# Loading ten triples of experts per layer in two parts instead of whole

## The reference

```python
scores = sigmoid(einsum('td,de->te', xf, router_w))          # 256 tokens, 64 experts
_, idx = top_k(scores + router_b, 6)
wts = sel / sum(sel) * 2.5                                   # sel: the six chosen scores
hid = silu(xb @ w_gate[e]) * (xb @ w_up[e])                  # w_gate, w_up: 1024 x 256
ys  = (hid @ w_down[e]) * w                                  # w_down: 256 x 1024
out = sum over a token's six experts + the shared expert
```

## Time and profile before

| | |
|---|---|
| median of 3 runs | 1425.58 us (1424.98 to 1426.55) |
| the profiled execution, its own time | 1425.3 us |
| its span, first to last instruction | 1423.5 us |
| TensorE matmul busy | 1266.5 us (89%) |
| HBM read | 496.57 MB |
| first layer's experts, about | 300 to 760 us |
| second layer's experts, about | 960 to 1416 us |

### The profile page before, as it was taken

One profiled execution on the slowest core, in us unless ns is written; L12 is line 12 of the kernel. 1 busy time (PEld: TensorE's weight loads), 2 busy tenths in 40 slices (PEclk: granted clock), 3 DMA queues, 4 the chain that ended last, 5 costly groups with the idle time before them and its releaser, 6 DMA issues.

```text
span 1423.5 us, 23092 instructions
## 1 busy us (share of the span) xinstructions
PE 1266.5 (89%) x9704; PEld 723.7 (51%) x9704; DVE 608.7 (43%) x1131; ACT 273.6 (19%) x464; POOL 59.9 (4%) x112
## 2 busy tenths in 40 slices
PE   5999888999998879888798999999999788977887
PEld 1445335775554444434446766875555344443444
DVE  5998872254433221222324687763433212222222
ACT  3226341321111110111112113131111101111111
POOL 0010581000000000000000000000000000000000
PEclk9999999999999999999999999989999999999999
DMA  9674865969999999999999962678999999999996
GB/s 380 241 206 88 161 196 213 392 262 395 422 423 421 430 429 426 427 428 428 423 417 344 390 261 89 240 336 333 401 423 421 422 432 428 426 428 428 427 422 271
DMA packets 54763, 502.85 MB, mean 353 GB/s; under 512 B 9788, under 2 KB 16700, under 8 KB 22588
## 3 DMA queue, kind: packets, MB, share of 16 engines
q1 hardware_dynamic: 54108, 499.18, 87.3%
q10 hardware_dynamic: 544, 2.10, 0.4%
HBM read 496.57 MB, written 4.69 MB: 352 GB/s over the span
## 4 chain that ended last, share of the span: by engine, by line
PE 54%; DMA 36%; DVE 6%; SPq 1%; issue 1%; ACT 1%; DVEq 0%; ACTq 0%
PE ps L790 52%; DMA arena<-in_w_experts 29%; DMA arena<-in_ada_w 7%; PE ps L461 2%; SPq L508 1%; ACT arena L1455 1%; DVE arena L2267 1%; DVE arena L2175 0%; DVE arena L1908 0%; PE ps L843 0%; DMA arena<-in_mcst 0%; DVE arena L1921 0%; PE ps L1055 0%; DVE arena L2257 0%; DVE arena L2256 0%
## 5 line engine op out<-in xcount | busy, mean ns | idle before, releaser
L790 PE MATMUL ps<-arena 128*32 128x512 f32 (+10 forms) x9192 | 1209.9, 457 | 137.9 <-DMA arena<-in_w_experts 55.0
L790 PEld LDWEIGHTS ps<-arena 128*32 128x32 f32 (+6 forms) x9192 | 691.8, 139 | 644.4 <-issue 493.8
L1455 ACT ACTIVATE arena<-ps 128x512 f32<-128x512 f32 (+6 forms) x261 | 142.1, 545 | 928.2 <-PE ps L790 880.5
L2117 DVE SCALAR_TENSOR_TENSOR arena<-arena,ps 128x256 f32<-128x256 f32 x44 | 21.1, 481 | 272.9 <-ACT arena L1455 272.9
L1455 ACT ACTIVATE arena<-arena 128x256 f32<-128x256 f32 (+7 forms) x143 | 94.0, 682 | 153.8 <-DVE arena L2135 58.2
L2133 DVE CAST arena<-ps 128x512 bf16<-128x512 f32 x42 | 29.0, 691 | 164.0 <-PE ps L790 164.0
L2077 DVE COPY arena<-ps 128x512 f32<-128x512 f32 x44 | 30.4, 691 | 132.2 <-PE ps L790 132.2
L2105 DVE TENSOR_TENSOR arena<-arena 128x1024 bf16<-128x1024 f32 x42 | 51.5, 1225 | 37.3 <-ACT arena L1455 37.0
L2135 DVE TENSOR_TENSOR arena<-ps,arena 128x1024 f32<-128x1024 f32 x42 | 51.4, 1224 | 1.4
L780 POOL MEMSET arena<- 128x1 f32 x2 | 0.2, 100 | 1165.3 <-PE ps L790 1165.3
L461 PE MATMUL ps<-arena 128*24 128x512 f32 x256 | 33.3, 621 | 3.3 <-DMA arena<-in_ada_w 3.3
(11 more groups left out here) (233 smaller groups left out, 471.1 us busy)
## 6 DMA issues: line engine op xcount, KB each, us to landing
arena<-in_w_experts SPq DMA_DIRECT2D x70, 3072.0 KB, 22.0
arena<-in_w_experts SPq DMA_DIRECT2D x80, 1024.0 KB, 13.1
arena<-in_w_experts SPq DMA_DIRECT2D x38, 2048.0 KB, 21.5
arena<-in_ada_w SPq DMA_DIRECT2D x34, 1024.0 KB, 6.8
arena<-in_ada_w SPq DMA_DIRECT2D x7, 2048.0 KB, 19.0
arena<-in_hy_w_in SPq DMA_DIRECT2D x6, 2048.0 KB, 15.4
arena<-in_w_experts SPq DMA_DIRECT2D x6, 1536.0 KB, 20.7
arena<-in_w_experts SPq DMA_DIRECT2D x18, 512.0 KB, 22.8
```

The costliest lines, as they stand in the source:

```text
L790: return pe.matmul(out, lhsT, rhs, start=start, stop=stop, skip_group_check=skip)
L1455: return act.activation(out, in_, func, **kw)
L2117: stt(hh, sg, wtab[:, n:n + 1], ps[:, GU, FF:2 * FF], M, M).then_inc(sem("h_done"), 1)
```

## The change

`whole(t)` is false for every triple. SP therefore takes the path of `half_loads` for triples 8 to 17 too, in both layers: 60 transfers of 3 MB become 60 of 2 MB and 60 of 1 MB. Bytes, slots, matrix products and the work of VectorE and ScalarE stay the same.

```diff
         def whole(t):
 
-            return LATE <= t < TRIPLES - 2
+            return False
```

## The result

Five runs after the change have a median of 1432.19 us (1431.16 to 1433.88); five of the kernel before, 1426.55. The ratio is 1.0035 with a 95% interval of 1.002 to 1.005: 5.0 us, 2.9 to 7.1 (it is estimated from all ten runs; the two medians alone are 5.6 us apart). The forecast was 1431.5 us, slower, in a range of 1428 to 1435.

What follows compares the result with a forecast made beforehand. The prediction took the full transfer queue, for which TensorE waits, as the bound. 3.0 us per layer gave 1425.3 + 6.0 = 1431.3 us profiled, and 1431.5 us as the median, in a range of 1428.0 to 1435.0.

Steps and rivals of the forecast that it cites:

- The queue sets the pace: Triples 9 to 17: transfers, not TensorE, set the 22.16 us per triple, so added transfer time reaches the end.
- the sum: Whole kernel: 3.0 us more per layer, both on the path, 6.0 us in all.
- The price by rates, 5.2 us, and by landings, 7.2: 60 split expert loads: 0.087 us each by window rates, 0.12 us each by landing intervals; 6.0 us taken in all.
- SP's issues and the earlier release cost and gain nothing: SP's queue: sixty more issues of 0.52 us are not waited for; earlier issues only join a full queue.
- The new wait before down products: TensorE, within a triple: down parts land 7.6 us after gate and up parts, with 1.8 us to spare; no cost.
- The lead is given back: Triples 8 to 17 start first products some 7.6 us earlier against the queue; not kept at triples 18 and 19.
- The start of triple 19 is set by the queue in both kernels: Last triple of each layer: waits for its weights before and after the change, with the same work following.
- Triple 19 near 748 and 1406: Last triple's start: about 3 us later in the first layer (748), 6 us later in the second (1406).
- No change (1): Split loads of triples 8 to 17: the parts cost nothing, 1425.6 to 1426.6 us; chance 13%.
- Holes in the queue (2): Start of whole triples: late whole loads starve the queue, so earlier issues make it faster, 1399.8 us; chance 6%.
- The interval of 23.51 us (3): Triples in parts: one slow interval in the second layer is the rule, much slower, 1452.6 us; chance 7%.
- The lower clock (4): Last triple of each layer: TensorE starts at the lower clock, 1.7 us more per layer, 1434.9 us; chance 9%.

Runs made afterwards that it cites:

- the padded rows: Kernel before, experts stored with padding so that one transfer moves two 12 KB pieces per partition: 1431.5 us against 1428.8, ratio 1.0031.
- two transfers: Kernel before, each whole load of triples 8 to 17 sent as an even-partition and an odd-partition transfer: 1429.06 us against 1428.8, ratio 1.0003.

## Why the prediction was right, step by step

- *The queue sets the pace.* Right: DMA share 1.01 after, and 22.47 in place of 22.16 us per triple; over 20 triples 6.2 us, near the 6.0 of the sum. The timed interval, 2.9 to 7.1 us, holds both.
- *The price by rates, 5.2 us, and by landings, 7.2.* The windows after give 422 GB/s, 3.146 / 0.422 = 7.455 us per expert and 0.097 more than whole: 5.8 us, between the two. The landings agree: from the last part of triple 7 to the last of triple 17, 30 experts took 221.99 and 221.21 us in the two layers before and 225.05 and 224.09 after, 5.9 us more (6.0 with the padded rows, 1.3 with two transfers). The sum stands. What the prediction left open was what in the change the price is of; the two runs that separate them show that it is the pieces of a partition's row, not the transfers.
- *SP's issues and the earlier release cost and gain nothing.* Right, and shown: sixty more issues with whole rows change nothing that shows, and neither does holding the parts back.
- *The new wait before down products.* Right. TensorE's waits for weights from 512 to 710 and from 1156 to 1354 (us, times, longest):

```profile
PE ps L790 <- DMA arena<-in_w_experts: 13.9, 8, 2.8
...
PE ps L790 <- DMA arena<-in_w_experts: 8.3, 5, 2.7
```

  The timeline has each of them at the start of a triple's gate and up products (0.35 at triple 10 to 1.02 at triple 17), none before down products.

- *The lead is given back.* Right: 8.88 and 8.51 us at triple 18.
- *"The start of triple 19 is set by the queue in both kernels."* This step was too sure. Triple 19 came when forecast, 748 and 1406, but without a wait: after its long wait triple 18's stretch took 14.29 and 14.83 us where it took 12.96, at a granted clock of 0.75 and 0.67 of full speed at its start, so partly at the lower of the two levels, 1.2 and 2.4 GHz. A window of each layer after:

```profile
729.60:735.00 5.40, 5.40 (x40) 1.49 (x44) 0.00 (x0) 0.00 (x0) 0.00 (x0) 0.75 1.02 425
1387.30:1393.00 5.70, 5.70 (x36) 1.45 (x40) 0.00 (x0) 0.00 (x0) 0.00 (x0) 0.67 1.03 423
```

  The same place of the second layer before:

```profile
1381.00:1386.00 5.00, 5.00 (x48) 1.56 (x52) 2.46 (x3) 1.06 (x1) 0.00 (x0) 1.00 1.03 424
```

  That used up the slack of 1.13 and 1.61 us before triple 19. The last part that triple 19's first products need was issued at 715.32 and 1373.40 and took 32.9 and 32.5 us to land, at 748.2 and 1405.9. In the first layer TensorE comes just as it lands, in the second some 0.5 us later. So in this execution about half a microsecond of the loss is TensorE's and the rest the queue's; had triple 18 been slower, it would have shown in the time.
- *Triple 19 near 748 and 1406.* That the instants fit to 0.4 us was partly luck. Triple 7 of the first layer, which the change does not reach, starts at 481.91 before and 481.92 after, but at 479.92 with the padded rows and at 485.04 with two transfers. The rates are the evidence; instants of single executions wander by more than the 3 us in question.
- *The rivals.* No change (1) is out by the interval and by 422 GB/s. Holes in the queue (2) were not there in this change; they exist earlier in the layer, as whole loads from triples 3 and 6 show. The interval of 23.51 us (3) was no rule: after the change one such stands in the second layer too (23.72 us, from 1274.49 to 1298.21), but the mean is 22.47. The lower clock (4) came, one triple earlier than rival 4 had it, and the slack hid most of what it cost: triple 19 itself followed without idling, and its 84 instructions and the 38 before them took 13.80 us, as 4.39 and 9.39 do at full speed.

## What to carry to other kernels

When transfers are the bound and the queue never runs dry, a load here cost its bytes plus a little for each contiguous piece of a partition, and nothing that shows for being one transfer more. So if such a load must be cut, try cutting it by partitions (here even and odd ones) before columns. Cutting by columns buys an earlier release of the slot; it pays where the compute engine is behind and the queue would run dry (from triple 3 on here; at triples 6 and 7 gain and loss about cancel), and only costs where the queue is full anyway. Look for the hole behind the loads that were changed, too. A lead that the next stage does not take over is given back, and the idle time it becomes can be followed by a lower clock just ahead of the end: here 8.5 to 8.9 us of waiting, then 0.67 to 0.75 of full speed.

## What was new about the hardware

A further piece of a row cost 0.08 to 0.1 us per expert of 128 partitions, even with pieces of 4 to 16 KB (427 to 428 GB/s with one piece of 24 KB, 422 to 423 with two, 414 with four); in the packet records it is 13 to 14 ns on the packet's engine, whatever the size from 4 to 24 KB. Splitting the same transfer over even and odd partitions left the rate at 427.
